# The context half of four norms' lo part: from VectorE to POOL

## The reference

```python
def rmsnorm(t, gain):
    tf = t.astype(jnp.float32)
    y = tf * lax.rsqrt(jnp.mean(tf * tf, axis=-1, keepdims=True) + EPS) * gain.astype(jnp.float32)
    return y.astype(t.dtype)

def modulate(t, gain, shift, scale):
    return rmsnorm(t, gain) * (1 + scale) + shift
...
        h = modulate(x, norm1_g[layer], sh1, sc1)
        hc = modulate(xc, norm1_g[layer], csh1, csc1)
        qkv, z, ba, sc_p, fn_u = split_cols(h @ w_in[layer], IN_SIZES)
        qkv_c, z_c, ba_c, sc_pc, fn_uc = split_cols(hc @ w_in[layer], IN_SIZES)
```

## Time and profile before

| | |
|---|---|
| median of 3 runs | 1926.28 us (1925.98 to 1929.57) |
| the profiled execution, its own time | 1927.05 us |
| its span, first to last instruction | 1925.3 us |
| mean granted TensorE clock | 0.967 of full speed |
| VectorE busy | 849.4 us in 1643 instructions |
| POOL busy | 484.9 us in 256 instructions |
| in the four norms of 512 tokens, VectorE's lo instructions | 64 of 128x256 |

### The profile page before, as it was taken

How to read it: one execution, slowest core, us unless ns; L and a number is a source line. 1 busy time by engine, 2 the same in 40 slices (tenths; PEclk the granted TensorE clock), 3 DMA queues, 4 the chain that set the end, 5 groups by cost and what they waited for, 6 DMA issues and landing times.

```text
span 1925.3 us, 34986 instructions
## 1 busy us (share of the span) xinstructions
PE 1802.2 (94%) x14968; PEld 1561.9 (81%) x14968; DVE 849.4 (44%) x1643; ACT 757.4 (39%) x1330; POOL 484.9 (25%) x256
## 2 busy tenths in 40 slices
PE   5998998888799999998999899999999989999998
PEld 3787997778689999787788677888888767689998
DVE  1647226566244333534477734221221346744343
ACT  3453532233335555522345334222222343755443
POOL 0136222121113443111134111121112211124443
PEclk7999999999899999899999899999999999999999
DMA  8443244232264554423211123323322336144553
GB/s 319 176 157 139 90 174 154 90 111 89 78 255 176 182 190 154 155 86 107 79 68 67 67 90 133 149 88 131 128 91 104 115 135 228 66 154 170 181 178 129
DMA packets 36584, 261.63 MB, mean 136 GB/s; under 512 B 4048, under 2 KB 4176, under 8 KB 6224
## 3 DMA queue, kind: packets, MB, share of 16 engines
q1 hardware_dynamic: 36432, 259.40, 37.4%
HBM read 258.34 MB, written 1.05 MB: 135 GB/s over the span
## 4 chain that ended last, share of the span: by engine, by line
PE 83%; DVE 8%; ACT 4%; issue 3%; DMA 2%; POOL 1%; SPq 0%; DVEq 0%; ACTq 0%
PE ps L876 20%; PE ps L878 19%; PE ps L877 19%; PE ps L927 3%; PE ps L903 2%; PE ps L893 1%; PE ps L1180 1%; PE ps L895 1%; PE ps L894 1%; PE ps L935 1%; PE ps L1168 1%; PE ps L1186 1%; PE ps L986 1%; PE ps L1019 1%; PE ps L1020 1%
## 5 line engine op out<-in xcount | busy, mean ns | idle before, releaser
L767 POOL TENSOR_TENSOR wl<-raw,wh 128x1024 fp32r<-128x1024 f32 (+1 forms) x179 | 426.6, 2384 | 1155.1 <-ACT wh L1583 1155.1
L876 PE MATMUL ps<-h_hi,wh 128*128 128x256 f32 (+1 forms) x1696 | 552.5, 326 | 4.9 <-POOL wl L767 4.2
L877 PE MATMUL ps<-h_lo,wh 128*128 128x256 f32 (+1 forms) x1696 | 547.5, 323 | 0.0
L878 PE MATMUL ps<-h_hi,wl 128*128 128x256 f32 (+1 forms) x1696 | 547.5, 323 | 0.0
L1583 ACT ACTIVATE wh<-raw 128x1024 fp32r<-128x1024 f32 (+1 forms) x330 | 342.2, 1040 | 401.1 <-PE ps L878 292.7
L876 PEld LDWEIGHTS ps<-h_hi,wh 128*128 128x128 f32 x1696 | 326.2, 192 | 31.7 <-POOL wl L767 5.3
L878 PEld LDWEIGHTS ps<-h_hi,wl 128*128 128x128 f32 x1696 | 326.0, 192 | 23.8
L877 PEld LDWEIGHTS ps<-h_lo,wh 128*128 128x128 f32 x1696 | 326.3, 192 | 23.3
L2100 DVE TENSOR_TENSOR wl<-raw,wh 128x1024 fp32r<-128x1024 f32 (+1 forms) x151 | 189.0, 1252 | 266.5 <-ACT wh L1583 266.2
L876 PE MATMUL ps<-gh,wh 128*128 128x256 f32 (+1 forms) x528 | 169.2, 320 | 0.0
L877 PE MATMUL ps<-gl,wh 128*128 128x256 f32 (+1 forms) x528 | 168.1, 318 | 0.0
(11 more groups left out here) (423 smaller groups left out, 2655.0 us busy)
## 6 DMA issues: line engine op xcount, KB each, us to landing
raw<-in_mod SPq DMA_DIRECT2D x72, 1024.0 KB, 4.9
raw<-in_ffn_in SPq DMA_DIRECT2D x66, 1024.0 KB, 4.8
raw<-in_ffn_out SPq DMA_DIRECT2D x24, 1024.0 KB, 4.8
raw<-in_w_in SPq DMA_DIRECT2D x16, 1024.0 KB, 4.8
raw<-in_w_gate SPq DMA_DIRECT2D x12, 1024.0 KB, 4.8
raw<-in_w_ab SPq DMA_DIRECT2D x12, 1024.0 KB, 4.9
raw<-in_ffn_out SPq DMA_DIRECT2D x12, 768.0 KB, 4.2
raw<-in_w_at SPq DMA_DIRECT2D x5, 1024.0 KB, 4.9
```

Of the source, the lines that this page charges most:

```text
L767: nc.gpsimd.tensor_tensor(wl[e % SPLIT][:, 0:entries[e]["words"]], part(e), wh[e % SPLIT][:, 0:entries[e]["words"]].bitcast(F32), ALU.subt ...
L876: nc.tensor.matmul(b[:, cols], wh[e % SPLIT][:, w], xh(k), start=(k == 0), stop=False)
L877: nc.tensor.matmul(b[:, cols], wh[e % SPLIT][:, w], xl(k), start=False, stop=False)
L878: ins = nc.tensor.matmul(b[:, cols], wl[e % SPLIT][:, w], xh(k), start=False, stop=(k == nk - 1))
```

## The change

POOL gets a function `norm_lo(name, idx)`. For each tile k it waits for VectorE's multiplication, writes `hraw` + shift of the context half into a ring of two tiles `ctxsum` (in the words of `spare`), waits for that instruction itself (`link`) and for ACT's hi, and subtracts `h_hi`, which counts up the new semaphore `<name>_hp`. It is called for a1, b1, b2 and c1, each time behind a call of `ahead` that makes the entries of the pair behind the norm. VectorE makes only the latent half's lo (`halves[-1:]`) and waits with the multiplication of tile k also for POOL's tile k - 4. TensorE waits in `dense_pair` for both counts, except in a2 and c2.

```diff
@@ build @@
+    ctxsum = sb("ctxsum", [P, 2, L], spare)
@@ POOL @@
         ahead = splitter(lo)
+
+        def norm_lo(name, idx):
+
+            lay, sec, cc = idx // 2, 3 * (idx % 2), slice(0, L)
+            for k in range(KD):
+                pool.wait_ge(sem(name + "_mul"), k + 1)
+                if k >= 2:
+                    pool.wait_ge(sem(name + "_hp"), k - 1)
+                link(nc.gpsimd.tensor_scalar(ctxsum[:, k % 2, :], hraw[:, k % 4, cc], mods[:, lay, 8 * sec + k, 1:2], None,
+                                             ALU.add))
+                pool.wait_ge(sem(name + "_hi"), k + 1)
+                nc.gpsimd.tensor_tensor(h_lo[:, k, cc], ctxsum[:, k % 2, :], h_hi[:, k, cc].bitcast(F32),
+                                        ALU.subtract).then_inc(sem(name + "_hp"), 1)
+
         nc.gpsimd.memset(cb[:], 0.0).then_inc(sem("cb_zero"), 1)
+        ahead("qkv", 0, depth=2)
+        norm_lo("a1", 0)
         for key in (("g1", 7), ("g2", 7)):
             ahead(*key)
...
         ahead("fo0", 3 * KD - 1)
+        ahead("rq", 0, depth=2)
+        norm_lo("b1", 2)
         full(pool, "fo0", 3 * KD - 1)
         nc.gpsimd.memset(vext[:, :, :, :, 64:65], 1.0).then_inc(sem("v_ones"), 1)
...
+        ahead("fa1", 0, depth=2)
+        norm_lo("b2", 3)
         ahead("fo1", 3 * KD - 1)
+        ahead("ak", 0, depth=2)
+        norm_lo("c1", 4)
         ahead("aq", 7)
@@ TensorE, dense_pair @@
                 pe.wait_ge(sem(name + "_h"), k + 1)
+                if name not in ("a2", "c2"):
+                    pe.wait_ge(sem(name + "_hp"), k + 1)
@@ VectorE, norm @@
                     if k >= 4:
                         dve.wait_ge(sem(name + "_h"), k - 3)
+                        if len(halves) == 2:
+                            dve.wait_ge(sem(name + "_hp"), k - 3)
...
                     dve.wait_ge(sem(name + "_hi"), i + 1)
-                    for r, cc in halves:
+                    for r, cc in halves[-1:]:
                         v = 0 if r is res_l else 1
                         ins = V.scalar_tensor_tensor(h_lo[:, i, cc], hraw[:, i % 4, cc],
```

## The result

The changed kernel takes **1941.55 us** (median; 1938.37 to 1951.03), the kernel before 1927.92: a ratio of 1.0079, with an interval of 1.0056 to 1.0101, so **13.6 us slower**. The forecast was 1928.1, the range ended at 1935.7: both were wrong, and the sign that got 0.24 is the one that came. The profiled execution took 1942.12 us (span 1940.3), against 1927.05 (1925.3) before. Two slow runs, one of e1_tt at 3490.3 us and one of the kernel before at 5786.2 us, stand in no median and no ratio.

A forecast was written before the change was run, and what follows sets the result against it. TensorE's matmuls bound the kernel (busy 94% of the span), so relieving VectorE pays only where TensorE waits for it. 0.8 + 0.3 + 0.4 + 0.3 = 1.8 us added gave 1928.1 us, range 1925.3 to 1935.7.

The forecast's parts named there:

- the sign that got 0.24: Whole kernel: slower by more than 3.9 us (0.2%), chance 0.24.
- Part 2: POOL's two added instructions per tile: copy 0.60, difference 0.73, with hand-overs 1.46 us per tile, alone.
- Rival 1: Norms' last tiles: TensorE waits for POOL, 1929.5 to 1935.7 us; chance 0.30, of which 0.24 beyond 3.9 us.
- Part 3: POOL and VectorE hold each other on SBUF: 0.07 to 0.24 per pair; period 1.56, in b1 1.66.
- the deadline: Last tile of each norm: a lo maker with a period under 11.24 / 7 = 1.60 per tile never holds TensorE.
- Part 1: VectorE loses one lo instruction per tile, some 12.5 us, lying under matmuls beyond the first tile: booked 0.
- Part 4: Starts of the norms: a1 later by 0.8 us, b1, b2 and c1 by 0.1 each.
- Part 5: POOL's queue: behind b1 the lo of the third rq weight entry comes late, +0.4 us; elsewhere nobody waits.
- Part 6: TensorE's 32 more semaphore waits in front of tiles: +0.3 us, bounds 0 and 1.6.

The follow-up runs named there:

- e1: Changed kernel with POOL's shifted copy as TENSOR_TENSOR, the shift broadcast as second input, in place of TENSOR_SCALAR: 1926.21 us, 0.9996 of the kernel before.
- e10: Changed kernel, but VectorE waits until POOL has made tile 7 of the norm before turning to its next weight entry: 1940.24 us, 1.0066.
- e6: Changed kernel, VectorE's latent lo of tiles 0 to 6 replaced by a same-size instruction with a PSUM input: 1939.47 us, 1.006.
- e4: Changed kernel, but ACT writes the shifted copy and POOL only takes the difference: 1932.32 us, 1.0027.
- e2: Changed kernel, but VectorE makes both lo halves again and POOL runs its two instructions into scratch nobody reads: 1942.33 us, 1.0085.
- e8: As e2, VectorE making both halves beside unread POOL work, but with the copy as TENSOR_TENSOR with broadcast column: 1950.18 us, 1.0116.
- e11: Changed kernel, copy with a constant in a1, plain copy in b2, two 128-column halves in c1, b1 as changed: one execution, 1949.79 us.
- e7: Changed kernel with POOL's shifted copy and its link done twice in each tile: 1968.77 us.
- e9: Changed kernel with the broadcast TENSOR_TENSOR copy and TensorE's two hi-by-hi matmuls of tile 0 ahead of the wait for lo: 1928.54 us, 1.0002.
- e5: Kernel before, with TensorE's two hi-by-hi matmuls of tile 0 ahead of the wait for lo: 1928.68 us, 1.001.

## Why the prediction was wrong, and where it was right

- **The step that failed is Part 2's price of the shifted copy.** It took 0.60 from L820, a two-input TENSOR_TENSOR whose second input changes rarely, and closed the range with 0.73, on the unspoken premise that one input can't cost more than two. It costs 0.92. As a TENSOR_TENSOR with a broadcast second input it does cost 0.61 (e1), so the row was read rightly, for an instruction that the kernel doesn't contain. The 0.05 of the hand-over to TensorE doesn't belong in the period either, for POOL's next copy doesn't wait for TensorE (e1: 1.45 with a holding of 0.07); that erred the other way. The period was 1.73 unheld, not 1.46, and 2.0 in the mean of b2's tiles, not 1.56, and that is over what TensorE's matmuls left it in every norm (1.60 in b2 and c1, 1.72 in a1, 1.77 in b1, by 12.01 / 7 and 12.38 / 7). With the copy at 0.61 and all the holding left in, the 13.6 us are gone (e1). Rival 1 had said what a price of 1.0 would do ("some +14"), and gave it no chance of its own. That its 14 is near the measured 13.6 is luck in part: the norms lost 11.8, some 2 of it by the weight entry that no term had, and the rest goes with the clock.
- **Part 3, the holding, was right per pair and incomplete.** Copies of 1.10 and 1.18 and a difference of 0.91 are 0.18 to 0.26 above unheld, near the upper one of the bounds, 0.07 to 0.24 per pair. The tile of 2.08 has two such holdings; over b2's tiles 1 to 4 (copies from 1171.82 to 1179.40) it is 0.17 per tile in the mean, for the 0.10 taken. Left out was that VectorE, relieved, comes to its next weight entry while POOL is still at tile 5 or 6, and holds it by 0.75 (the 1.48 above): 0.7 us in b2 and in c1 (e10). Of b2's 2.6, then, some 0.8 is the unheld period, 0.7 to 1.0 the weight entry and the rest VectorE's lo (e6, e10). None of it would count with the deadline kept: in e1 the last difference is held even longer (1.64), and tile 7 is on time. In b1 every copy but the last is held, and POOL's period is 1.89 where 1.66 was forecast. The holding in it, 1.89 less 1.73 or 0.16, is not over the 0.20 that was taken for two pairs: the excess is the copy's price (POOL in b1):

```profile
803.54 1.10 POOL L781 TENSOR_SCALAR ctxsum<-hraw,mods 128x256 f32<-128x256 f32 x1
804.72 0.74 POOL L784 TENSOR_TENSOR h_lo<-ctxsum,h_hi 128x256 fp32r<-128x256 f32 x1
805.43 1.09 POOL L781 TENSOR_SCALAR ctxsum<-hraw,mods 128x256 f32<-128x256 f32 x1
```

- **Part 1 was right:** the relief of VectorE is worth nothing by itself; e1 and e4 have it with a maker in time, and neither is faster than before. What it does is keep VectorE from being the late one (e2 and e8 against the changed kernel and e1).
- **Part 4.** a1's start was to cost 0.8; it cost 1.4 (11.05 against 9.68), since the copy costs 0.92 and copy (1.09) and difference (0.89) were both held. In all five kernels that move the copy and the lo to POOL in a1 (the changed kernel, e1, e6, e10, e11) it is 1.0 to 1.7 longer than that 9.68, e7 and e9 aside. The other starts were to cost 0.1 each: 0.19 in b2, and in c1 where the clock is nearly whole (6.19 in e1 and e10). POOL's rows at a1, and VectorE's lo that holds the difference:

```profile
44.50 2.51 POOL L768 TENSOR_TENSOR wl<-raw,wh 128x1024 fp32r<-128x1024 f32 x1 [42.39 <-ACT wh L1608]
47.00 1.09 POOL L781 TENSOR_SCALAR ctxsum<-hraw,mods 128x256 f32<-128x256 f32 x1
48.17 0.89 POOL L784 TENSOR_TENSOR h_lo<-ctxsum,h_hi 128x256 fp32r<-128x256 f32 x1
```

```profile
48.00 0.47 DVE L2185 SCALAR_TENSOR_TENSOR h_lo<-hraw,mods,h_hi 128x256 fp32r<-128x256 f32 x1
```

- **Part 5's place was right, its size small beside the rest:** behind b1 TensorE waits 0.70 for the weight entry that POOL makes late (the row at 813.64 above); 0.4 was forecast, with a shorter norm ahead of it.
- **Part 6:** no cost in b2 where 0.3 was taken for all (e1, tile 7 at 11.21).
- **The method of the deadline held.** A maker with 1.45 (e1) stops TensorE once, for 0.16 in c1, and one with a copy of 0.39 (e11, b2) leaves the dense part at its 12.60; with 1.72 and one entry in the way, tile 7 comes where 7 periods put it (e6: 13.01).
- The Trainium skill (GPSIMD Engine Reference, section 4.1) was cited for the copy near line rate. The runs don't contradict it for COPY, 0.39 for 256 columns, what the prediction has for VectorE's instructions of that size, and do for TENSOR_SCALAR, 0.92; the measurement decides. Its other rule (SBUF — State Buffer, "two separate sides") of an exclusive lock is borne out again, by a 0.73 on POOL that lasts 1.48 beside VectorE's 1.23 and ends 0.57 behind it.

## What to carry to other kernels

Price an instruction by rows of its own opcode on its own engine: fewer inputs is no upper bound. If the trace has no such row, let the range reach past the nearest one, and work out what the sum does there; here 0.3 us per instruction was the whole result, because the moved work sat within 10% of a deadline. When work goes to an engine that is held by the one it comes from, as POOL and VectorE hold each other here, ask for both: what the maker's period becomes, and what the relieved engine will start early and lay in its way.

## What the runs showed of the hardware that I had not expected

- On POOL, 128x256 in fp32 costs 0.92 as TENSOR_SCALAR with a pointer, 0.84 with a constant, 0.73 as TENSOR_TENSOR with two full inputs, 0.61 with a broadcast second one, and 0.39 as COPY.
- POOL's work on SBUF costs the kernel 14 to 22 us even when nothing waits for it (e2, e8), while VectorE instructions with an input in PSUM pass it unhurt (L2172 in e8: 0.47 in b2, under POOL's work).
- A start of the dense part 0.9 to 1.1 earlier in b2 is worth 0.4 (e5) or nothing (e9) there, and nothing that the whole kernel's time shows, when the makers' period stays.
- The kernel before scatters over 20 us from run to run, along with its mean granted clock (0.955 to 0.972), while the dense parts of b2 and c1 repeat to 0.02 us between two executions.
